# First three expert lists and gathers made in the route stage; the shared expert's second product made in the second norm; four tile buffers there

## The reference, cut to what matters

```python
for l in range(DEPTH):                                   # DEPTH = 2
    mix = hybrid_mixer(x, ...)
    x = layer_norm(DN_ALPHA * x + mix, ln1_g[l], ln1_b[l])
    ffn = moe_ffn(x, ...)
    x = layer_norm(DN_ALPHA * x + ffn, ln2_g[l], ln2_b[l])

def moe_ffn(...):
    scores = sigmoid(xf @ router_w)
    _, idx = top_k(scores + router_bias, 8)              # of 64
    gates = scores at idx, divided by their sum, * ROUTED_SCALE
    # per expert, for its tokens: y = (silu(h @ w1) * (h @ w3)) @ w2, times the gate
    routed = sum of each token's eight y                 # w1, w3: 1024x256; w2: 256x1024
    shared = (silu(xf @ sw1) * (xf @ sw3)) @ sw2         # sw1, sw3: 1024x256; sw2: 256x1024
    return routed + shared
```

## Time and profile before

| | |
|---|---|
| median of three runs | 2444.59 us |
| the profiled execution's own time | 2440.64 us |
| its span | 2438.5 us |
| mean granted clock of TensorE | 0.955 of full speed |
| busy: TensorE / VectorE / ScalarE / GpSimd | 90% / 66% / 56% / 22% |
| moved by the DMA engines | 580.22 MB, mean 238 GB/s |
| expert stage of the first layer | about 446 to 1158 us |
| second norm of the first layer | about 1162 to 1229 us |

### The profile page before, as it was taken

The page is one execution under the profiler, slowest core; times in us unless marked ns, Lnnn a source line. Parts: engine busy times, 40 slices in busy tenths (PEclk is TensorE's granted clock), DMA queues, the critical chain, the costliest instruction groups (busy, mean ns, idle before and its releaser), DMA issues. The chain is left out here.

```text
span 2438.5 us, 31605 instructions
## 1 busy us (share of the span) xinstructions
PE 2185.7 (90%) x10840; PEld 1588.3 (65%) x10840; DVE 1610.5 (66%) x2260; ACT 1354.0 (56%) x1754; POOL 543.2 (22%) x310
## 2 busy tenths in 40 slices
PE   6999999799998998998679999997989899989956
PEld 5788756576676766665266886565766676766632
DVE  2583323588888877886545923246978788878847
ACT  3534631387777767676034355215867777767731
POOL 0001000242343333332000010003433333333310
PEclk9899999899999999999789999998999999999988
DMA  6213040699999999996721230408999999999965
GB/s 192 77 44 147 1 169 26 191 353 338 343 347 337 349 333 349 339 332 246 293 85 52 65 127 1 177 18 282 356 339 343 346 346 337 348 341 327 341 232 244
DMA packets 141434, 580.22 MB, mean 238 GB/s; under 512 B 40292, under 2 KB 65124, under 8 KB 88856
## 3 DMA queue, kind: packets, MB, share of 16 engines
q1 hardware_dynamic: 96280, 511.73, 58.3%
q0 software_dynamic: 45056, 67.22, 8.9%
HBM read 555.19 MB, written 61.37 MB: 253 GB/s over the span
## 5 line engine op out<-in xcount | busy, mean ns | idle before, releaser
L1193 POOL DMA_INDIRECT y_rows<-y,index x128 | 290.6, 2271 | 822.6 <-ACT y L1424 796.1
L1246 PE MATMUL ps_up<-w_hi,rowsT_hi 128*100 128x512 f32 x1024 | 422.0, 412 | 27.9 <-issue 19.0
L1248 PE MATMUL ps_up<-w_hi,rowsT_lo 128*100 128x512 f32 x1024 | 405.4, 396 | 0.0
L1390 ACT CAST w_hi<-w_other 128x2048 fp32r<-128x2048 f32 x128 | 245.7, 1920 | 184.7 <-DMA w_other<-exp_w 171.5
L1390 ACT CAST w_hi<-w 128x2048 fp32r<-128x2048 f32 x128 | 245.2, 1917 | 150.8 <-DMA w<-exp_w 87.0
L1327 DVE TENSOR_TENSOR w_lo<-w,w_hi 128x2048 fp32r<-128x2048 f32 x128 | 292.2, 2284 | 27.6 <-ACT w_hi L1390 27.5
L1327 DVE TENSOR_TENSOR w_other_lo<-w_other,w_hi 128x2048 fp32r<-128x2048 f32 x128 | 292.0, 2282 | 6.8 <-ACT w_hi L1390 6.7
L1271 PE MATMUL ps_y<-w_hi,hiddenT_hi 128*100 128x512 f32 x512 | 214.2, 418 | 74.3 <-issue 70.2
L1185 POOL DMA_INDIRECT rows<-x_rows,index x128 | 202.2, 1580 | 334.0 <-DVE index L1312 278.4
L1246 PEld LDWEIGHTS ps_up<-w_hi,rowsT_hi 128*100 128x100 f32 x1024 | 173.9, 170 | 86.0 <-issue 33.6
L1332 DVE TENSOR_TENSOR w_lo<-w,w_hi 128x2048 fp32r<-128x2048 f32 x96 | 219.1, 2283 | 2.7 <-ACT w_hi L1397 2.7
(11 more groups left out here) (228 smaller groups left out, 4135.6 us busy)
## 6 DMA issues: line engine op xcount, KB each, us to landing
w<-exp_w SPq DMA_DIRECT2D x232, 1024.0 KB, 15.1
w_other<-exp_w SPq DMA_DIRECT2D x128, 1024.0 KB
w_first<-exp_w SPq DMA_DIRECT2D x34, 1024.0 KB, 9.2
got<-y_rows SPq DMA_DIRECT2D x8, 4096.0 KB, 12.8
wbuf<-w_in SPq DMA_DIRECT2D x16, 1024.0 KB, 5.6
w_out_sb<-w_out SPq DMA_DIRECT2D x2, 4096.0 KB, 19.2
bias<-bias_tiles SPq DMA_DIRECT2D x2, 2560.0 KB, 9.0
sh_w<-sh_w SPq DMA_DIRECT2D x4, 1024.0 KB, 9.0
```

Of the source, the lines that this page charges most:

```text
L1193: pool.indirect_dma_start(d["y_rows"], bass.IndirectOffsetOnAxis(ap=index[0:CAP, x.step, 1:2], axis=0), y[0:CAP, x.slot, :], None, bounds_ ...
L1246: pe.matmul(ps_up[b][0:CAP], hi, w_hi, start=(k == 0), stop=False)
L1248: mm = pe.matmul(ps_up[b][0:CAP], lo, w_hi, start=False, stop=(k == KD - 1))
L1390: act.copy(w13_hi[:, :, k, :], w13[x.slot][:, :, k, :]).then_inc(S["up_hi_b" if half else "up_hi_a"], 1)
```

## The change

In the route stage, the positions are made as soon as the mask is there, in the middle of the shared expert's first product; then the lists of experts 0 to 2 (`hots`, `pick`, `indices`) and their gathers are made. The shared expert's second product and the accumulation leave the stage; x is only scaled by ALPHA. In the expert stage, every step makes the list and the gather of three experts on, the last three of them for a next pass; `posm` is lowered three steps before the end for it. SyncE no longer waits for the gathers. `y` has two buffers in place of four. In the second norm, TensorE makes the shared product (weights loaded there first) and adds x for all four tiles ahead of the first sum of places; each tile has buffers of its own in SBUF and PSUM, and is loaded in two halves.

```diff
@@ _mix_and_route: GpSimd, TensorE
                 pool.wait_ge(S["rows_cleared"], 1)
+                pool.wait_ge(S["x1_out"], 16 * NT)
+                for k in range(FIRST):
+                    pool.wait_ge(S["index_ready"], k + 1)
+                    pool.indirect_dma_start(sb["rows"][0:CAP, k, :], None, d["x1_rows"],
...
+                for k in range(FIRST):
+                    pool.wait_ge(S[f"rows{k}_in"], 16)
...
                 shared_up(1, 0, early)
-                shared_up(3, 0, early)
-                for q in (0, 2, 1, 3):
-                    shared_up(q, early, SEQ).then_inc(S["up_made"], 1)
                 pe.wait_ge(S["mask_ready"], 1)
...
-                pe.wait_ge(S["gated"], 2)
-                for t in range(NT):
-                    if t >= 2:
-                        pe.wait_ge(S["acc_ready"], t - 1)
-                    for c in range(2):
-                        for m in range(2):
-                            mm = pe.matmul(dn_bank[t % 2][:, c * 512:(c + 1) * 512], act_out[:, m, t * P:(t + 1) * P],
-                                           w2[:, m, c * 512:(c + 1) * 512], start=(m == 0), stop=(m == 1))
-                    mm.then_inc(S["down_made"], 1)
+                shared_up(3, 0, early)
+                for q in (0, 2):
+                    shared_up(q, early, SEQ).then_inc(S["up_made"], 1)
+                pe.wait_ge(S["tables"], 1)
+                pick(0)
+                pick(1)
+                for q in (1, 3):
+                    shared_up(q, early, SEQ).then_inc(S["up_made"], 1)
+                pick(2)
@@ _mix_and_route: VectorE
+                hots(0)
+                hots(1)
+                indices(0)
+                hots(2)
+                indices(1)
+                hots(3)
+                gated(0)
+                indices(2)
                 step(dve.tensor_reduce(cnt[:, 0:1], ps_c[:, 0:NE], AX.X, ALU.max))
...
+                gated(1)
...
                 for t in range(NT):
-                    dve.wait_ge(S["down_made"], t + 1)
-                    dve.scalar_tensor_tensor(out=x_sb[:, t, :], in0=x_sb[:, t, :], scalar=ALPHA, in1=dn_bank[t % 2],
-                                             op0=ALU.mult, op1=ALU.add).then_inc(S["acc_ready"], 1)
+                    o = dve.tensor_scalar(x_sb[:, t, :], x_sb[:, t, :], ALPHA, None, ALU.mult)
+                o.then_inc(S["scaled"], 1)
+                dve.wait_ge(S["scaled"], 1)
@@ _experts
-        y = T("y", [P, SLOTS, D])
+        y = T("y", [P, 2, D])
...
-                sp.wait_ge(S["dma_turns"], 3)
...
@@ _second_norm: SyncE, TensorE
+                sp.dma_start(w2[:], d["sh_w2"][bass.ds(l, 1)].rearrange("o (m p) c -> p (o m) c", p=P)).then_inc(S["shared_in"], 16)
                 for t in range(NT):
-                    if t >= 2:
-                        sp.wait_ge(S["row_sum"], t - 1)
-                    sp.dma_start(got[:, t % 2], y[t]).then_inc(S[f"y{t}_in"], 16)
+                    sp.dma_start(got[:, t, 0:HALF], y[t, :, 0:HALF]).then_inc(S[f"y{t}a_in"], 16)
+                    sp.dma_start(got[:, t, HALF:TOPK], y[t, :, HALF:TOPK]).then_inc(S[f"y{t}b_in"], 16)
...
+                pe.wait_ge(S["shared_in"], 16)
                 for t in range(NT):
-                    pe.wait_ge(S[f"y{t}_in"], 16)
-                    if t >= 2:
-                        pe.wait_ge(S["row_sum"], t - 1)
                     for c in range(2):
                         cols = slice(c * 512, (c + 1) * 512)
-                        pe.matmul(ps[t % 2][:, cols], ident, x[:, t, cols], start=True, stop=False)
+                        for m in range(2):
+                            pe.matmul(ps[t][:, cols], sb["shared"][:, m, t * P:(t + 1) * P], w2[:, m, cols], start=(m == 0), stop=False)
+                        pe.matmul(ps[t][:, cols], ident, x[:, t, cols], start=False, stop=False)
+                for t in range(NT):
+                    pe.wait_ge(S[f"y{t}a_in"], 16)
+                    for c in range(2):
+                        cols = slice(c * 512, (c + 1) * 512)
                         for s in range(HALF):
-                            mm = pe.matmul(ps[t % 2][:, cols], ident, got[:, t % 2, s, cols], start=False, stop=(s == HALF - 1))
+                            mm = pe.matmul(ps[t][:, cols], ident, got[:, t, s, cols], start=False, stop=(s == HALF - 1))
                     mm.then_inc(S["summed"], 1)
```

More of the change, by code:

```diff
@@ L838, in _mix_and_route @@
         up_bank = [flat_a[:, 0:512], flat_a[:, 512:1024], ps_mix[:, 0:512], ps_mix[:, 512:1024]]
-        dn_bank = [flat_x, flat_a]
+        hot, index, expert_gate = sb["hot"], sb["index"], sb["gate"]
+        number, absent = sb["number"][:], sb["ones"]
         with nc.Block() as block:
@@ L1028, in _, with hots, indices, gated @@
                 dve.tensor_tensor(parts[:, :, :, DEST_LOW], place[:], parts[:, :, :, DEST], ALU.subtract).then_inc(S["tables"], 1)
-                for m in range(2):
+                dve.wait_ge(S["pos_made"], 1)
+                posm = sb["posm"]
+                step(dve.scalar_tensor_tensor(out=posm[:], in0=ps_r[:, 1], scalar=NOT_ROUTED, in1=mask[:],
+                                              op0=ALU.add, op1=ALU.mult))
+                step(dve.tensor_scalar(posm[:], posm[:], NOT_ROUTED, None, ALU.subtract))
+                def hots(k):
+                    if k >= 2:
+                        dve.wait_ge(S["picked_made"], k - 1)
+                    dve.tensor_tensor(hot[:, k % 2], number.unsqueeze(1).to_broadcast([P, NT, CAP]),
+                                      posm[:, :, k:k + 1].to_broadcast([P, NT, CAP]), ALU.is_equal).then_inc(S["hot_ready"], 1)
+                def indices(k):
+                    dve.wait_ge(S["picked_made"], k + 1)
+                    got = flat_x[0:CAP, (k % 2) * 512:(k % 2) * 512 + PART]
+                    dve.tensor_reduce(expert_gate[0:CAP, k:k + 1], got[:, GATES:GATES + 3], AX.X, ALU.add)
+                    with nc.allow_low_precision(reason="sums of two whole numbers below 2**14"):
+                        dve.tensor_reduce(index[0:CAP, k, :], got[:, 0:GATES].rearrange("p (v q) -> p v q", q=2),
+                                          AX.X, ALU.add).then_inc(S["index_ready"], 1)
+                def gated(m):
                     dve.wait_ge(S["silu_out"], m + 1)
@@ L1067, in __init__ @@
         self.known = isinstance(lap, int)
+        self.expert = self.n % NE if self.known else self.n
     def __add__(self, k):
@@ L1071, in __add__, with n_at_least @@
         return Turn(self.lap + s // LAP, s % LAP)
+    def n_at_least(self, k):
+        return not self.known or self.n >= k
     def has(self, k):
@@ L1193, in put @@
                     pool.indirect_dma_start(d["y_rows"], bass.IndirectOffsetOnAxis(ap=index[0:CAP, x.step, 1:2], axis=0),
[L1194 to L1198, removed]
+                                            y[0:CAP, x.slot % 2, :], None, bounds_check=PLACES - 1, oob_is_err=False
+                                            ).then_inc(S[f"y{x.slot % 2}_out"], 16)
                 def step(x):
@@ L1202, in step @@
                         put(x + -2)
-                    if x.has(3):
-                        gather(x + 3)
+                    gather(x + FIRST)
                 _laps(pool, step)
@@ L1207, in _ @@
                 put(LAST)
-                for s in range(SLOTS):
-                    pool.wait_ge(S[f"y{s}_out"], 16 * (NE // SLOTS))
+                for s in range(2):
+                    pool.wait_ge(S[f"y{s}_out"], 16 * (NE // 2))
+                for s in range(FIRST):
+                    pool.wait_ge(S[f"rows{s}_in"], 16 * (NE // SLOTS))
             @block.tensor
@@ L1226, in turn_rows @@
                 def turn_rows(x):
-                    pe.wait_ge(S[f"rows{x.slot}_in"], 16 * x.times(SLOTS))
+                    if x.n_at_least(FIRST):
+                        pe.wait_ge(S[f"rows{x.slot}_in"], 16 * (x.times(SLOTS) - (1 if x.slot < FIRST else 0)))
                     if x.has(-1):
@@ L1274, in down @@
                     mm.then_inc(S["down_made"], 1)
-                for k in range(3):
-                    pick(Turn(0, k))
                 turn_rows(Turn(0, 0))
                 def step(x):
-                    if x.has(3):
-                        pick(x + 3)
+                    pick(x + FIRST)
                     up(x, 0)
@@ L1360, in step @@
                 def step(x):
[L1361 to L1364 removed]
+                    if x.known and x.n + FIRST + 1 == NE:
+                        next_pass()
+                    hots(x + (FIRST + 1))
+                    indices(x + FIRST)
                     if x.has(-1):
```

145 lines of the change are left out of this document (73 added, 72 removed).

## The result

The changed kernel took 2423.09 us (median of five runs, 2422.48 to 2427.98); the kernel before, on the same chip, 2442.73 (median of five). The ratio is 0.9934, with a 95% interval of 0.9919 to 0.995: a gain of about 16 us, between 12 and 20. The direction was right and 10.2 was forecast. As a gain, 16 lies inside the forecast's own range of 4 to 17. As a time it does not: 2434.4 was forecast, and 2423.09 lies 4.9 us under that range (2428 to 2441) and 0.9 under the wider one with the rivals (2424 to 2447), because the forecast started from 2444.59, and every later series of the kernel before has a lower median.

What follows compares the result with a forecast made beforehand. The expert stage was taken to end when its weights have come, plus a compute tail. Per layer -12.7 us up to the second norm and +7.6 in it, twice, gave -10.2 from 2444.59: 2434.4 us, range 2428 to 2441 (2424 to 2447 with rivals).

Steps and rivals of the forecast that it cites:

- the rivals: Three other outcomes: third gather held behind scalings (0.18), norm sums not delayed (0.08), TensorE at half clock (0.12).
- Block end: Route stage: the third gather's landing ends the block at 437.4 and no longer at 444.56, -7.1 us a layer.
- landing price: Route stage's third gather: lands 4.7 us after issue because the DMA is idle; under load the shortest took 9.7.
- First load: Expert stage: first weight load about 10.7 us earlier, by -7.1 from the route stage and -3.6 from SyncE's wait on gathers.
- Inside the expert stage: First weight load to last scatter: -2.6 us from three gathers fewer, +0.6 for extra lists at the end, per layer.
- Second norm: Tile 0's r waits for TensorE's front products, 35.4 us after the first load's issue; net +7.6 us per layer.
- Rival 2: Second norm: sums not delayed, norm runs at VectorE's pace, -5 us per layer, total -35, 2409 us; chance 0.08.
- Rival 3: Second norm: all 24 front products at half clock, +17.5 us per layer, +35 in total, 2469 us; chance 0.12.
- y with two buffers: Expert stage: ScalarE's scaling waits for the scatter two experts back, with 5.4 us to spare, so cost 0.
- The sign that I named: Expert stage: the profile after should show no wait of ScalarE's y for a scatter.
- The port lock: VectorE's two-port operations keep GpSimd from writing descriptors; the trace's 5.32 us gather beside VectorE's low halves was said to agree.

Runs made afterwards that it cites:

- product alone: Kernel before with the shared product moved, y with two buffers and the new second norm; lists stay in the expert stage: 2433.56 us, ratio 0.9972.
- lists alone: Changed kernel with the shared product back in the route stage behind the third list, and the old second norm: 2434.43 us, 0.998 of the kernel before.
- tile by tile: Changed kernel with each tile's shared products and x right ahead of that tile's sums in the second norm: 2403.74 us, 0.9854 of the kernel before.
- x first: Changed kernel, second norm: x added first, each tile's sums ahead of its shared products, w2 loaded behind tile 0: 2403.82 us, 0.9858 of the kernel before.
- scalings ahead: Changed kernel with VectorE's four scalings of x ahead of the third index; one execution for its trace, total not compared; first load 27.4 us after the mask.

## Why the prediction was right, and where its size was off

**Block end, forecast 437.4, measured 436.4.** The chain of estimates held at each joint: third gather issued at 431.77 (432.7), landing 4.6 (4.7), scalings 2.50 us (2.6, between 1.7 and 3.4), VectorE done at 435.45 (436.5). Some of the 1.0 us is not the chain's: the mask came 0.4 us sooner in this execution. The landing price was the choice that mattered, 4.7 of an idle DMA and not 9.7 under load, and the three gathers landed in 4.6 to 5.8.

**First load -10.7, measured -11.1 and -10.6.** The sum is right, and so are its two terms: the block ends 7.8 us sooner after the mask (7.1), and from there to the first load it is 3.3 less (3.6). But the two terms do not belong to the two halves of the change as they look. With the product alone moved, the start already came 9.9 us earlier (26.0 on average over the layers against 35.9), though SyncE still waits for the third gather's turn. The lists added 0.8 to 1.0: what they save SyncE inside the expert stage, the route stage pays as a wait for the gathers' landing. Their gain lies behind that: TensorE starts 32.1 us after the mask in place of 34.3 and 33.6 with the product alone, and the stage seems shorter, as follows.

**Inside the expert stage, forecast -2.0 (-2.6 + 0.6).** Of the terms this is the one that is furthest off, if any is. From first load to last scatter the four layers with the lists inside (before, product alone) took 702.8, 700.0, 702.8 and 697.1, mean 700.7; the twelve of the changed kernel in its two profiles, lists alone, tile by tile, x first and scalings ahead average 697.4. That is about -3.2, 1.2 more than I said, or 2.4 us in all; but the four values lie up to 5.7 us apart and the twelve up to 6.0, so 1.2 is not clear of the scatter. The gathers' DMA time was the only gain I had counted; TensorE's earlier start and four fewer lists in VectorE's way are candidates for the rest, if there is one. No run separates them.

**Second norm, forecast +7.6, measured +7.2 and +7.7.** `r` of tile 0 came at 35.0 us (35.4), waiting for TensorE, and the norm took 73.4 and 74.1 us (74). Rival 2, by which the front products would be hidden, is refuted by the wait of 11.76. Its gain is there to be had, but it takes another order of the same instructions: tile by tile it is 63.3 us. Rival 3's half clock did not last: the granted clock is 0.50 for the first 4 us or so and 1.00 from 1158 on. The 32 products up to `r` took 30.0 us (1152.38 to 1182.43, hand-over included), 2.6 more than 32 x 0.857, where I had charged 3.1 + 0.2.

**y with two buffers, 0.** The sign that I named, no wait for a scatter, failed once. In layer 1 of the changed kernel ScalarE's last scaling waits 4.1 us for the scatter two experts back, which was issued at 2322.31 and landed 10.4 later. The same wait, 4.1 to 4.7 us, stands at the end of one layer or both in all but one of the other traces with two buffers. My sum used the shortest period in the middle of the stage, 9.7 us; the last three scalings start only 7.2 and 5.4 us apart. It cost at most 0.3 us: the product that this scaling needs ended at 2332.52, and the scaling started at 2332.82.

**The sum.** By the trace: -10.9 at the start, -2.75 inside, +7.4 in the norm, -6.25 a layer, 12.5 of the 12.7 us between the two profiled executions. My sum of the same terms was 10.2. What is left to the median's 16 is 3.4 us between the profiled executions and the medians, of the size in which one layer's expert stage varies from run to run; I cannot assign it. The forecast was anchored on 2444.59, the median of three runs of before; over 15 and 26 further runs before has medians of 2439.42 and 2439.69.

**The halves against the whole.** Product alone saves 6.8 us, lists alone 4.9, together 11.7; the whole saves 16.1 (12.9 to 19.3). By the intervals the difference, 4.4, is at the edge of what can be told, and the profiled executions do not show it: there the halves save 7.9 and 9.0 us, and the whole 12.7 and 14.3. What the traces do show is the start of the loads: 9.9 us sooner with the product alone, 2.1 later with the lists alone, and 10.9 sooner with both. With the product still in the route stage the lists delay its end. Without the product they end the block 2.5 us later than the product alone does (22.5 us after the mask in place of 20.0), and save SyncE its wait of 3.8 us.

**The port lock.** The earlier trace rows show a gather of 5.32 us beside VectorE's low halves, and I wrote that it ends when they do, and took it as agreeing with the lock by two-port operations. Both are wrong. The low halves end at 455.06 and the gather at 456.01, 0.95 later; with the product alone, 445.93 and 446.89, again 0.96. In layer 1 of both kernels the gather took 5.45 and ended 0.95 and 0.94 after them. And these low halves are `tensor_tensor` with two inputs in SBUF. The expert stage shows more. Here are one gather that began while a low half ran, and one that began just ahead of one (kernel before):
```profile
506.17 2.28 DVE L1327 TENSOR_TENSOR w_lo<-w,w_hi 128x2048 fp32r<-128x2048 f32 x1
506.64 2.76 POOL L1185 DMA_INDIRECT rows<-x_rows,index  x1 [0.69 <-issue]
...
1014.49 1.07 POOL L1185 DMA_INDIRECT rows<-x_rows,index  x1 [0.31 <-issue]
1014.52 2.30 DVE L1327 TENSOR_TENSOR w_lo<-w,w_hi 128x2048 fp32r<-128x2048 f32 x1
```
Of that kernel's 128 gathers, 34 began while a low half ran (one of them at its very start, 0.01 ahead), and all 34 ended 0.94 to 0.96 after its end, about a whole issue (1.06 us alone). Another 31 began 0.01 to 0.98 ahead of a low half, and all of them took 1.07 or 1.08: a low half does not hold a gather that is already under way. The scalings do: begun 0.56 and 0.60 ahead of them, a gather was held until 0.13 and 0.14 after the last.

The Trainium skill, SBUF — State Buffer, in the box on VectorE blocking DMA, has the two-port operation lock GpSimd out of descriptor writing, and the section "A bandwidth-pool intuition that's wrong" says "blocked until DVE-end + ~115 ns": beside the scalings the 0.13 and 0.14 agree. Its section "Who interferes with whom" has a VectorE instruction with two SBUF inputs contend only with GpSimd's reads, and infers that descriptor writing goes on. The trace agrees with that too, where nothing already begun was held; what is held is the start of a gather, and it can be long (4.3 us beside two low halves). That the held part is the gather's read of its index list from SBUF would fit, but no run shows it.

## What to carry to other kernels

Work moved off a crowded boundary must be placed, not just appended: the 24 products (16 shared and 8 of x) cost 7.4 us a layer at the head of TensorE's in-order queue, and with each tile's products ahead of its own sums the norm is 3.0 us shorter than before the change. Ask of each first consumer what stands ahead of it in the queue, and of the second as well, since whatever saves the first tile may only lengthen the wait for the next. And a long wait on an engine that waits for its loads anyway is a small price: one y buffer gave ScalarE 269 us of waits for scatters and cost the kernel about 9 us (nothing in some executions, 11 to 18 in others). A room to spare that is worked out from the middle of a stage need not hold at its end.

## What the runs showed of the hardware

- An indirect gather's issue on GpSimd, 1.06 us alone, took 3.18 and 3.23 us when 2.49 us of back-to-back float32 `tensor_scalar` of 128x1024 began 0.56 and 0.60 us after it. It landed 7.6 and 7.1 us after its issue in place of 5.3 and 5.1.
- A gather issued while float32 `tensor_tensor` of 128x2048 with both inputs in SBUF ran ended 0.94 to 0.96 us after it, in 34 cases of 34 in the kernel before (one of them issued 0.01 ahead), and took 2.6 to 5.5 us. One issued 0.03 us or more ahead of such an operation took 1.07 or 1.08, in 30 of 30.
- In-place float32 `tensor_scalar` of 128x1024: 2.50 us for four, 0.62 each, against 0.43 for 128x512.
- A pause of TensorE of 2.42 us (with the lists alone, in both layers) was followed by eight records of 5.37 us in place of 3.60: the granted clock was 1.00 up to it and 0.50 for about 3.4 us after it, so even a short idle stretch was followed by slow products.
